# A hybrid attention layer on one core: VectorE scales a tile's attention output at the head of the next tile's queue

## The chip, the core and the metric

The kernel runs on one core of one Trainium2 chip. Five engines work side by side, each through its own queue in order: TensorE (PE, matrix products and transposes; its weight loads are shown as PEld), VectorE (DVE), ScalarE (ACT), GpSimd (POOL), and SyncE (SP), which issues nearly all DMAs. They meet only at semaphores. The metric is the device time of one execution in microseconds (us), lower is better.

## The reference, cut to what matters

The layer takes 2048 tokens of width 1024. A first projection gives queries, keys, values and an indexer; the indexer scores every earlier key, each query keeps its 256 best, and eight heads of width 64 attend over those alone. A pooling mixer, an output projection, a squared-ReLU MLP and a gated embedding follow. The part around the change is:

```python
score = jnp.einsum('bqh,bqhs->bqs', wb, jax.nn.relu(logits))
score = jnp.where(causal[None], score, -jnp.inf)
_, sel = lax.top_k(score, n_keep)                 # n_keep = 256
...
s = jnp.einsum('bqgrd,bqkgd->bqgrk', qg, kg) * ATTN_SCALE
pr = jax.nn.softmax(s, axis=-1)
o = jnp.einsum('bqgrk,bqkgd->bqgrd', pr, vg)      # attention output
mix = jnp.concatenate([attn_out, pool_out], axis=-1) @ w_o[i]
h = h + rmsnorm(mix, g_mix_post[i])
```

## The kernel before, in words

There are three stages, one after the other: the projection, the attention stage (about 427 to 1836 us of the trace) and the MLP with the rest. The change is in the attention stage.

The attention stage goes over 16 tiles of 128 queries, numbered i = 0 to 15. Tile i attends over its first 128(i+1) keys, cut into 1 block of keys for tiles 0 to 3, 2 for tiles 4 to 7, 3 for tiles 8 to 11 and 4 for tiles 12 to 15 (`blocks_of`). Each tile has eight heads; H = 8i + h counts them through. Every engine has its own loop over H, written out in full. There is no scheduler: the order of the code is the order of each queue.

For each head TensorE makes the scores of head H+2 or H+3 (lines 1455 and 1456, `exact_product`), turns the probabilities of head H block by block (line 1506, `turn_probs`), and multiplies them with the values (line 1520, `weigh`). All eight heads of a tile add their output into one bank of PSUM, bank 7. In head 0 of a tile it also turns the queries of the next tile (line 1468, `turn_queries`). Its product for block b stands one block behind the turn: turn 0, turn 1, weigh 0, turn 2, weigh 1 and so on; the last weigh of a head is behind the scores of head H+3.

Scores, turned queries and indexer products share a ring of three PSUM banks. An item can be written when the item three places before it was taken out (`wait_ring`). With three blocks or more per head, the scores of one head fill the ring, so the next item waits until VectorE has taken that head's first block out. The fourth block of head H+2 is the first ring item of head H; after it come, in head 0, the two halves of the turned queries.

VectorE takes the score blocks out with the mask added and their maximum (line 1112, `mask_head`), makes the negated maximum (line 1117), and splits the turned queries (line 1079, `split_queries`), before which TensorE can't make the scores that come next in the ring. In between VectorE and ScalarE search the threshold of the 256th best score for a pair of later tiles: 32 rounds of bisection per pair, three per head, from head 0 of an even tile to head 2 of the odd tile behind it (none in tiles 14 and 15). In a round VectorE counts for one tile (line 1131, `count_exact`) and ScalarE for the other (line 831, `count_below`), and then VectorE moves the threshold (lines 1139 to 1148, `move_threshold`; line 1129 prepares the next value). ScalarE does its first count behind its copy of the second turned block (line 880), or behind the first one where there is only one block.

`outputs(i)` is what the change moves. It waits for the last weigh of tile i (semaphore `pv_ps`), takes the reciprocal of the eight sums (line 1190), and scales bank 7 into `o_sb` (line 1192). Only then can TensorE write bank 7 for tile i+1: its first weigh of a tile waits for `o_rdy`. `o_sb` is turned in head 3. `scale_mix(i-2)`, in the same head 0, scales the output projection of the tile before last (line 1206); it waits for a root that GpSimd makes (line 680), and GpSimd's residual addition (line 689) waits for it.

Of the kernel before, what the change touches and what calls it, by code (L numbers as in the profile page):

```python
# [47 lines left out]
def hybrid_block(nc, x, p, positions, g_mix_pre, w_in, w_pool, pool_scale, w_o, g_mix_post,  # L48
# [29 lines left out]
    with ExitStack() as ctx:  # L78
# [276 lines left out]
        def turns_index(H):  # L355

            i, h = divmod(H, Q_HEADS)
            return (i + 3, i + 4) if i % 2 == 1 and h == 4 and i + 4 < T else ()
# [23 lines left out]
        for H in range(HEADS):  # L382
            i, h = divmod(H, Q_HEADS)
# [25 lines left out]
        def rounds_in(H):  # L409

            i, h = divmod(H, Q_HEADS)
            s = Q_HEADS * (i % 2) + h
            if i // 2 + 1 >= T // 2 or s > 10:
                return range(0)
            return range(min(3 * s, ROUNDS), min(3 * s + 3, ROUNDS))
# [24 lines left out]
        def over(cols, width):  # L440

            return cols.unsqueeze(2).to_broadcast([P, cols.shape[1], width])
# [537 lines left out]
        def _(dve):  # L980
# [93 lines left out]
            def split_queries(i):  # L1074
                low = slice(P // 2, P)
                for n in range(2):
                    dve.wait_ge(q_hi, 2 * i + n + 1)
                    part = q_parts[low, i % 2, 4 * n:4 * n + 4, :]
                    nc.vector.tensor_tensor(part, split4(bank[low, ring_bank("q", i, n), :]), part.bitcast(F32),  # L1079
                                            ALU.subtract).then_inc(ring_done, 1)  # L1080
# [22 lines left out]
            def mask_head(H):  # L1103

                i, h = divmod(H, Q_HEADS)
                if h == 0 and i >= FIRST_PICK:
                    dve.wait_ge(mask_rdy, i - FIRST_PICK + 1)
                if H >= 3:
                    dve.wait_ge(pT_ps, head_first[H - 2])
                for b, (o, w) in enumerate(blocks[i]):  # L1110
                    dve.wait_ge(ring_ps, ring[("s", H, b)] + 1)
                    nc.vector.tensor_tensor_reduce(out=probs[:, H % 3, o:o + w], in0=bank[:, ring_bank("s", H, b), 0:w],  # L1112
                                                   in1=mask[:, i % 2, o:o + w], scale=1.0, scalar=LEAST, op0=ALU.add,
                                                   op1=ALU.max, accum_out=block_max[:, H % 2, b:b + 1]).then_inc(ring_done, 1)
                nb = len(blocks[i])
                dve.wait_ge(ring_done, ring[("s", H, nb - 1)] + 1)
                nc.vector.tensor_reduce(neg_max[:, h:h + 1], block_max[:, H % 2, 0:nb], AX_X, ALU.max,
                                        negate=True).then_inc(negmax_rdy, 1)

            def start_search(t):  # L1120
                nc.vector.memset(threshold[:], 0).then_inc(thr_rdy, 1)
                dve.wait_ge(score_rdy, t - FIRST_PICK + 1)

            def count_exact(t, k):

                keys = P * (t + 1)
                dve.wait_ge(thr_rdy, tries(t) + k + 1)
                if k > 0:
                    nc.vector.tensor_scalar(next_tried[:], threshold[:], 2 ** (31 - k) // 2, None,
                                            ALU.bitwise_xor).then_inc(tried_rdy, 1)  # L1130
                nc.vector.tensor_scalar(kept[:, 0:keys], score[:, 0, 0:keys], threshold[:, 0:1].bitcast(F32), -float(P),  # L1131
                                        ALU.is_lt, ALU.add, accum_out=below[:, 0:1]).then_inc(exact_count, 1)

            def move_threshold(t, k):

                done = ROUNDS * (t // 2 - 1)
                dve.wait_ge(exact_count, done + k + 1)
                dve.wait_ge(act_count, done + k + 1)
                nc.vector.tensor_scalar(too_few[:], below[:], float(P * (t + 2) - 2 * KEEP), None,  # L1139
                                        ALU.is_gt).then_inc(few_rdy, 1)  # L1140
                dve.wait_ge(few_rdy, done + k + 1)
                if k == 0:
                    nc.vector.tensor_scalar(flip[:], too_few[:], -1.0, None, ALU.mult).then_inc(flip_rdy, 1)
                    dve.wait_ge(flip_rdy, t // 2)
                    nc.vector.tensor_scalar(threshold[:], flip[:], 1 << 30, None, ALU.bitwise_xor).then_inc(thr_rdy, 1)
                else:
                    dve.wait_ge(tried_rdy, (ROUNDS - 1) * (t // 2 - 1) + k)
                    nc.vector.scalar_tensor_tensor(out=threshold[:], in0=too_few[:], scalar=31 - k, in1=next_tried[:],  # L1148
                                                   op0=ALU.logical_shift_left, op1=ALU.bitwise_xor).then_inc(thr_rdy, 1)

            def settle(t):

                keys = P * (t + 1)
                dve.wait_ge(thr_rdy, tries(t) + ROUNDS + 1)
                nc.vector.tensor_scalar(kept[:, 0:keys], score[:, 1, 0:keys], threshold[:, 1:2].bitcast(F32), 0.0,
                                        ALU.is_gt, ALU.add, accum_out=above[:, 1:2]).then_inc(settle_step, 1)
                nc.vector.tensor_scalar(next_up[:], flip[:, 1:2], 2.0, 1.0, ALU.mult, ALU.add).then_inc(settle_step, 1)
                dve.wait_ge(settle_step, 2 * (t // 2))
                nc.vector.scalar_tensor_tensor(out=toggled[:], in0=above[:, 1:2], scalar=float(KEEP), in1=next_up[:],
                                               op0=ALU.is_ge, op1=ALU.mult).then_inc(settled, 1)  # L1160
# [26 lines left out]
            def outputs(i):  # L1187
                dve.wait_ge(pv_ps, head_first[Q_HEADS * (i + 1)])
                dve.wait_ge(oT_ps, i)
                nc.vector.reciprocal(inv_denom[:], denom[:, i % 2, :]).then_inc(invden_rdy, 1)  # L1190
                dve.wait_ge(invden_rdy, i + 1)
                nc.vector.tensor_tensor(o_sb[:], bank[:, 7, :].rearrange("p (h d) -> p h d", d=HEAD),
                                        over(inv_denom[:], HEAD), ALU.mult).then_inc(o_rdy, 1)
# [5 lines left out]
            def scale_mix(i):  # L1199
                dve.wait_ge(rstdB_rdy, 2 * i + 1)  # L1200
                dve.wait_ge(h2_st, 16 * i)
                if i == 0:
                    dve.wait_ge(wo_ld, 16 * (K + 1))
                for n in range(2):
                    cols = slice(n * 512, (n + 1) * 512)
                    nc.vector.scalar_tensor_tensor(out=h2_t[:, cols], in0=bank[:, n, :], scalar=rstdB[:, 0:1],
                                                   in1=g_post_row[:, cols], op0=ALU.mult, op1=ALU.mult).then_inc(h2_scaled, 1)
# [19 lines left out]
            for H in range(HEADS):  # L1227
                i, h = divmod(H, Q_HEADS)
                rounds = rounds_in(H)
                first = 2 * (i // 2) + 2  # L1230
                if len(rounds) and rounds[0] == 0:
                    start_search(first)
                if len(rounds):
                    count_exact(first, rounds[0])
                if H + 2 < HEADS:
                    mask_head(H + 2)
                if h == 0 and i >= 1:
                    outputs(i - 1)
                if h == 0 and i >= 2:
                    scale_mix(i - 2)  # L1240
                for k in rounds:
                    if k != rounds[0]:
                        count_exact(first, k)
                    move_threshold(first, k)
                if i % 2 == 1 and h == 3 and i + 2 < T:
                    settle(i + 2)
                    select(i + 1)
                if i % 2 == 1 and h == 4 and i + 2 < T:
                    select(i + 2)
                if h == 0 and i + 1 < T:  # L1250
                    split_queries(i + 1)
                for t in turns_index(H):
                    split_index_queries(t)
                weigh_heads(index_share(H))
                if h == 1 and i >= 2:
                    residual_mean(i - 2)
                if h == 7 and i >= 1:
                    mix_mean(i - 1)
# [424 lines left out]
```

## Time and profile before

| | |
|---|---|
| time, median of 3 runs | 3635.95 us (3632.55 to 3638.81) |
| profiled execution | 3635.46 us, its span 3633.7 us |
| PE busy | 3153.3 us, 87% |
| DVE busy | 1671.5 us, 46% |
| ACT busy | 1314.5 us, 36% |
| POOL busy | 351.8 us, 10% |
| attention stage, 427 to 1836 us | PE 1064.08, DVE 906.76, ACT 719.03 us of 1409 |
| mean granted TensorE clock | 0.79 of full speed in the attention stage, 0.98 behind it |

The shares are averages over the three stages. In the attention stage no engine is busy all the time; what is to be read there is who waits for whom around the start of each tile.

### The profile page before, as it was taken

How to read it: one execution, taken by the hardware profiler on the slowest of the kernel's cores; microseconds unless marked ns; L12 is line 12 of the kernel's file. 1: busy time of each engine (PE TensorE's matmuls, PEld its weight loads, DVE VectorE, ACT ScalarE, POOL GpSimd, SP SyncE). 2: the span in 40 equal slices, each digit the busy share in tenths (PEclk: the TensorE clock that was granted, in tenths of full speed). 3: DMA queues.
4: the chain of work that ended last, by engine and by line, in shares of the span. 5: the costliest groups of instructions: out<-in, count | busy, mean ns of one | idle time of the engine just before them, and what ended most of it. 6: DMA issues, size and time to landing. Idle time of an engine off the chain costs nothing.

```text
span 3633.7 us, 38370 instructions
## 1 busy us (share of the span) xinstructions
PE 3153.3 (87%) x13944; PEld 2422.5 (67%) x13944; DVE 1671.5 (46%) x3354; ACT 1314.5 (36%) x2130; POOL 351.8 (10%) x457
## 2 busy tenths in 40 slices
PE   5999667677777777788869999999999999999998
PEld 4888545455565666667658885688857888478873
DVE  3221277767677777752133334333343333433333
ACT  3222255637373746633332222222223222232221
POOL 1323311120303012000000000000000000000000
PEclk9999867777878878788889999999999999999999
DMA  3111211110101000000053332233313333032210
GB/s 111 52 52 52 93 41 38 43 36 27 33 27 32 12 27 27 21 21 21 27 191 116 94 103 72 75 121 100 122 35 105 99 98 122 29 121 94 93 58 23
DMA packets 211405, 241.93 MB, mean 67 GB/s; under 512 B 57504, under 2 KB 158368, under 8 KB 211232
## 3 DMA queue, kind: packets, MB, share of 16 engines
q1 hardware_dynamic: 208928, 231.27, 20.1%
q10 hardware_dynamic: 2304, 8.39, 0.6%
q8 instruction: 104, 1.70, 0.2%
q14 instruction: 69, 0.57, 0.1%
HBM read 203.98 MB, written 35.65 MB: 66 GB/s over the span
## 4 chain that ended last, share of the span: by engine, by line
issue 54%; PE 25%; DVE 10%; ACT 7%; POOL 2%; DMA 1%; SPq 0%; DVEq 0%; POOLq 0%; ACTq 0%
PE bank L1409 9%; PE bank L1538 6%; PE bank L1520 4%; DVE kept L1131 3%; ACT drop L831 2%; PE bank L1455 2%; ACT probs L865 2%; PE bank L1456 2%; PE bank L1506 1%; POOL score L700 1%; ACT probsT L880 1%; DVE kept L1178 1%; DVE too_few L1139 1%; DVE probs L1112 1%; DVE threshold L1148 1%
## 5 line engine op out<-in xcount | busy, mean ns | idle before, releaser
L1274 DVE TENSOR_TENSOR w_lo<-w_raw,w_hi 128x1024 fp32r<-128x1024 f32 x256 | 312.7, 1222 | 522.2 <-ACT w_hi L923 516.5
L1520 PE MATMUL bank<-values,probsT 128*128 128x64 f32 x2176 | 368.6, 322 | 130.4 <-ACT probsT L880 125.7
L1520 PEld LDWEIGHTS bank<-values,probsT 128*128 128x128 f32 x2176 | 354.1, 239 | 176.4 <-ACT probsT L880 163.6
L923 ACT CAST w_hi<-w_raw 128x1024 fp32r<-128x1024 f32 x256 | 267.3, 1044 | 563.1 <-PE bank L1409 535.0
L1409 PE MATMUL bank<-hn_hi,w_hi 128*128 128x512 f32 x1024 | 401.0, 392 | 16.1 <-DVE hn_lo L1291 10.9
L1409 PE MATMUL bank<-w_hi,hid_lo 128*128 128x512 f32 x1024 | 406.4, 397 | 0.0
L1409 PE MATMUL bank<-w_lo,hid_hi 128*128 128x512 f32 x1024 | 406.4, 397 | 0.0
L1409 PE MATMUL bank<-w_hi,hid_hi 128*128 128x512 f32 x1024 | 406.4, 397 | 0.0
L1409 PE MATMUL bank<-hn_lo,w_hi 128*128 128x512 f32 x1024 | 400.1, 391 | 0.0
L1409 PE MATMUL bank<-hn_hi,w_lo 128*128 128x512 f32 x1024 | 400.0, 391 | 0.0
L880 ACT COPY probsT<-bank 128x384 f32<-128x384 f32 (+3 forms) x320 | 163.6, 518 | 558.6 <-PE bank L1506 558.2
L831 ACT ACTIVATE drop<-score,threshold 128x512 bf16<-128x512 f32 (+6 forms) x224 | 305.5, 1364 | 89.7 <-DVE threshold L1148 66.0
L1131 DVE TENSOR_SCALAR_CACHE_REDUCE kept<-score,threshold 128x384 f32<-128x384 f32 (+6 forms) x224 | 315.1, 1407 | 1.0
L1455 PE MATMUL bank<-k_hi,q_parts 128*128 128x384 f32 (+3 forms) x320 | 170.0, 531 | 148.1 <-DVE q_parts L1079 87.5
L1112 DVE CUSTOM_DVE_ANT_0 probs<-bank,mask 128x384 f32<-128x384 f32 (+3 forms) x320 | 183.5, 607 | 149.2 <-PE bank L1456 148.4
L1538 PE MATMUL bank<-wo_sb,mixT_t 128*128 128x512 f32 x512 | 245.9, 632 | 0.7 <-ACT mixT_t L837 0.7
L1409 PEld LDWEIGHTS bank<-hn_hi,w_hi 128*128 128x128 f32 x1024 | 193.1, 189 | 58.0 <-issue 17.5
L1655 PE MATMUL bank<-w_gate_sb,h3T 128*128 128x512 f32 x512 | 226.8, 602 | 0.0
L1409 PEld LDWEIGHTS bank<-w_hi,hid_hi 128*128 128x128 f32 x1024 | 193.2, 189 | 46.6
L1409 PEld LDWEIGHTS bank<-w_lo,hid_hi 128*128 128x128 f32 x1024 | 193.2, 189 | 46.6
L1409 PEld LDWEIGHTS bank<-w_hi,hid_lo 128*128 128x128 f32 x1024 | 193.2, 189 | 46.6
L1309 DVE CAST hid_hi<-square 128x512 fp32r<-128x512 f32 x128 | 54.6, 427 | 365.3 <-ACT square L948 365.3
(173 smaller groups left out, 4610.5 us busy)
## 6 DMA issues: line engine op xcount, KB each, us to landing
w_raw<-in_w_up SPq DMA_DIRECT2D x64, 1024.0 KB, 5.5
w_raw<-in_w_down SPq DMA_DIRECT2D x64, 1024.0 KB, 5.0
x_in<-in_x SPq DMA_DIRECT2D x16, 512.0 KB, 4.6
q_t<-q_scratch SPq DMA_DIRECT2D x32, 256.0 KB, 3.7
x_t<-in_x SPq DMA_DIRECT2D x16, 512.0 KB, 4.3
h_scratch<-h_t SPq DMA_DIRECT2D x16, 512.0 KB, 3.1
hnT_scratch<-hn2T_t SPq DMA_DIRECT2D x16, 512.0 KB, 3.5
hn_lo<-hnT_scratch SPq DMA_DIRECT2D x4, 2048.0 KB, 11.8
```

The source lines that it names most:

```text
L831: nc.scalar.activation(drop[:, 0:keys], score[:, 1, 0:keys], ACT.Sign, scale=-1.0, bias=threshold[:, 1:2].bitcast(F32), accum_out=below[:, ...
L865: nc.scalar.activation(span, span, ACT.Exp, bias=neg_max[:, h:h + 1], accum_out=denom[:, i % 2, h:h + 1]).then_inc(exp_rdy, 1)
L880: nc.scalar.copy(probsT[:, m % 2, 0:w], bank[:, 5 + m % 2, 0:w]).then_inc(pT_ev, 1)
L923: nc.scalar.copy(w_hi[:, p % 4, :].rearrange("p (k f) -> p k f", f=piece_width(p)), raw_piece(p)).then_inc(w_hi_rdy, 1)
L1112: nc.vector.tensor_tensor_reduce(out=probs[:, H % 3, o:o + w], in0=bank[:, ring_bank("s", H, b), 0:w], in1=mask[:, i % 2, o:o + w], scale= ...
L1131: nc.vector.tensor_scalar(kept[:, 0:keys], score[:, 0, 0:keys], threshold[:, 0:1].bitcast(F32), -float(P), ALU.is_lt, ALU.add, accum_out=b ...
L1274: nc.vector.tensor_tensor(out_p, raw_piece(p), hi_p.bitcast(F32), ALU.subtract).then_inc(w_lo_rdy, 1)
L1409: ins = nc.tensor.matmul(dst, lhs[a], rhs[b], start=(first and n == 0), stop=(last and n == 2))
L1455: nc.tensor.matmul(dst, q, k_hi[:, key, o:o + w], start=True, stop=False)
L1520: last = nc.tensor.matmul(bank[:, 7, h * HEAD:(h + 1) * HEAD], probsT[:, m % 2, a * P:(a + 1) * P], values[:, kt, HEAD * kv:HEAD * (kv + 1 ...
L1538: last = nc.tensor.matmul(bank[:, n, :], mixT_t[:, k, :], wo_sb[:, k, n * 512:(n + 1) * 512], start=(k == 0), stop=(k == K - 1))
L1655: last = nc.tensor.matmul(bank[:, (2, 4)[n], :], h3T[:, a % 2, k, :], w_gate_sb[:, k, n * 512:(n + 1) * 512], start=(k == 0), stop=(k == K ...
```

## The change

In head 0 of each tile from tile 1 on, `outputs(i - 1)` is issued ahead of the first count and of the masked maxima of head H+2, where it was issued behind them. The final `outputs(15)` and every other engine's queue stay as they are.

```diff
                 if len(rounds) and rounds[0] == 0:
                     start_search(first)
+                if h == 0 and i >= 1:
+                    outputs(i - 1)
                 if len(rounds):
                     count_exact(first, rounds[0])
                 if H + 2 < HEADS:
                     mask_head(H + 2)
-                if h == 0 and i >= 1:
-                    outputs(i - 1)
                 if h == 0 and i >= 2:
                     scale_mix(i - 2)
                 for k in rounds:
```

This is VectorE's queue at the start of tile 10, an even tile with three blocks of 384, 512 and 512 keys. The rows with a minus and a plus are the same work, in its place before and now; h_t stands for the tile of the residual stream.

```order
 L1197 TENSOR_SCALAR msB<-ssB 128x1
 L1121 MEMSET threshold 128x2
-L1131 TENSOR_SCALAR kept,below<-score,threshold 128x1664
-L1112 ISA probs,block_max<-bank,mask 128x384
-L1112 ISA block_max 128x1
-L1117 TENSOR_REDUCE neg_max<-block_max 128x1
...
 L1190 RECIPROCAL inv_denom<-denom 128x8
 L1192 TENSOR_TENSOR o_sb<-bank,inv_denom 128x512
+L1131 TENSOR_SCALAR kept,below<-score,threshold 128x1664
+L1112 ISA probs,block_max<-bank,mask 128x384
```

The reciprocal and the scaling now stand ahead of the count of 1664 scores and of the three blocks of head 82.

In tile 14 there is no search. VectorE's queue at its start is now:

```order
1897 L1197 TENSOR_SCALAR msB<-ssB 128x1
1898 L1190 RECIPROCAL inv_denom<-denom 128x8
1899 L1192 TENSOR_TENSOR o_sb<-bank,inv_denom 128x512
1900 L1112 ISA probs,block_max<-bank,mask 128x384
1901 L1112 ISA block_max 128x1
1902 L1112 ISA probs,block_max<-bank,mask 128x512
1903 L1112 ISA block_max 128x1
```

Rows 1898 and 1899 stood behind the four blocks of head 114 and their negated maximum, and stand ahead of them now.

TensorE's queue at the same place, which the change leaves as it was. The first row is the last weigh of tile 13, the third the fourth score block of head 114, the fifth the queries of tile 15:

```order
1677 L1520 MATMUL bank<-values,probsT 128x64 x4
1678 L1506 MATMUL bank<-ident,probs 128x128 x3
1679 L1455 MATMUL bank<-k_hi,q_parts 128x512
1680 L1456 MATMUL bank<-k_lo,q_parts 128x512
1681 L1468 MATMUL bank<-ident,q_t 128x128 x8
1682 L1506 MATMUL bank<-ident,probs 128x128 x4
1683 L1520 MATMUL bank<-values,probsT 128x64 x3
```

Nothing moved here: rows 1679 and 1681 wait for ring banks that line 1112 empties, row 1683 for `o_sb`.

## Rows read from the trace of the kernel before

**Rows 1.** The page: the group of line 1112; busy us, mean ns, idle before.

```profile
L1112 DVE CUSTOM_DVE_ANT_0 probs<-bank,mask 128x384 f32<-128x384 f32 (+3 forms) x320 | 183.5, 607 | 149.2 <-PE bank L1456 148.4
```

**Rows 2.** The tile inv_denom: durations in ns (least, median, most), and who waited.

```profile
L1190 DVE RECIPROCAL inv_denom<-denom x16: 202/203/204, 481.2 to 1796.2; 128x8 f32<-128x8 f32 x16
L1192 DVE TENSOR_TENSOR o_sb<-bank,inv_denom x16: 691/692/692, 481.4 to 1796.4; 128x512 f32<-128x512 f32 x16
...
  PE bank L1520: 3.0, 4
```

**Rows 3.** Who waited for whom: us in total, times, longest.

```profile
PE bank L1455 <- DVE q_parts L1079: 87.5, 16, 7.9
```

**Rows 4.** Timeline, start of tile 10: start, us busy, engine, line; in brackets the idle time before.

```profile
1166.37 1.00 PE L1520 MATMUL bank<-values,probsT 128*128 128x64 f32 x8
1166.01 1.95 DVE L1131 TENSOR_SCALAR_CACHE_REDUCE kept<-score,threshold 128x1664 f32<-128x1664 f32 x1
1168.59 1.17 PE L1468 MATMUL bank<-ident,q_t 128*128 128x128 f32 x8 [0.89 <-DVE block_max L1112]
1170.02 0.69 DVE L1192 TENSOR_TENSOR o_sb<-bank,inv_denom 128x512 f32<-128x512 f32 x1
1170.62 1.40 DVE L1206 SCALAR_TENSOR_TENSOR h_t<-bank,rstdB,g_post_row 128x512 f32<-128x512 f32 x2
1172.10 2.35 POOL L689 TENSOR_TENSOR h_t<-h_t,x_t 128x1024 f32<-128x1024 f32 x1 [1.84 <-DVE h_t L1206]
1172.71 1.77 DVE L1139 TENSOR_SCALAR too_few<-below 128x2 int32<-128x2 f32 x1 [0.69 <-ACT drop L831]
```

**Rows 5.** Timeline, starts of tiles 8, 12 and 4.

```profile
972.54 1.00 PE L1520 MATMUL bank<-values,probsT 128*128 128x64 f32 x8
972.29 1.68 DVE L1131 TENSOR_SCALAR_CACHE_REDUCE kept<-score,threshold 128x1408 f32<-128x1408 f32 x1
975.76 0.69 DVE L1192 TENSOR_TENSOR o_sb<-bank,inv_denom 128x512 f32<-128x512 f32 x1
976.57 1.41 DVE L1206 SCALAR_TENSOR_TENSOR h_t<-bank,rstdB,g_post_row 128x512 f32<-128x512 f32 x2
...
1383.70 1.00 PE L1520 MATMUL bank<-values,probsT 128*128 128x64 f32 x8
1383.46 2.21 DVE L1131 TENSOR_SCALAR_CACHE_REDUCE kept<-score,threshold 128x1920 f32<-128x1920 f32 x1
1392.20 0.78 DVE L1139 TENSOR_SCALAR too_few<-below 128x2 int32<-128x2 f32 x1 [1.67 <-ACT drop L831]
...
645.86 1.00 PE L1520 MATMUL bank<-values,probsT 128*128 128x64 f32 x8
646.27 1.15 DVE L1131 TENSOR_SCALAR_CACHE_REDUCE kept<-score,threshold 128x896 f32<-128x896 f32 x1
649.95 1.41 DVE L1206 SCALAR_TENSOR_TENSOR h_t<-bank,rstdB,g_post_row 128x512 f32<-128x512 f32 x2 [0.66 <-POOL rstdB L680]
```

**Rows 6.** Timeline, start of tile 13.

```profile
1505.17 0.67 DVE L1139 TENSOR_SCALAR too_few<-below 128x2 int32<-128x2 f32 x1 [1.78 <-ACT drop L831]
```

**Rows 7.** Timeline, starts of tiles 14 (three rows) and 15.

```profile
1609.27 0.56 DVE L1112 CUSTOM_DVE_ANT_0 probs<-bank,mask 128x384 f32<-128x384 f32 x1 [3.60 <-PE bank L1456]
1610.63 1.25 PE L1520 MATMUL bank<-values,probsT 128*128 128x64 f32 x8
1614.60 0.85 PE L1520 MATMUL bank<-values,probsT 128*128 128x64 f32 x6 [0.62 <-DVE o_sb L1192]
...
1710.38 1.08 PE L1520 MATMUL bank<-values,probsT 128*128 128x64 f32 x8 [1.49 <-DVE o_sb L1192]
```

**Rows 8.** Stretches of tiles 12 and 15: engine times, granted clock (1.00, 0.50), DMA.

```profile
1385.00:1386.20 1.20, 0.03 (x1) 0.00 (x0) 1.20 (x5) 1.13 (x2) 1.06 (x2) 0.86 0.00 0
1386.20:1388.00 1.80, 1.79 (x6) 1.49 (x7) 1.45 (x5) 1.02 (x2) 1.43 (x3) 0.50 0.00 0
1710.40:1712.00 1.60, 1.60 (x15) 1.60 (x16) 1.15 (x2) 0.74 (x4) 0.38 (x1) 1.00 0.00 0
```

## The prediction

> **What bounds the kernel now.** I read the waits first, then the timeline around the start of every tile. All durations are from the profiled execution: span 3633.7 us, device time 3635.46 us, 0.5 below the median of 3635.95. The sum is a difference, so I add it to the median.
>
> The product that the change wants to release is the first weigh of a tile. TensorE waited for `o_sb` 4 times, 3.0 us in all [rows 2]; that is the whole prize. The large wait at the same place is another: for the split queries, 16 times, 87.5 us, the longest 7.9 [rows 3]. In head 0 VectorE splits them behind all three rounds of the search, so until then TensorE stands, whatever happened to bank 7. The start of a tile is therefore paced by VectorE's queue, with ScalarE's counts in it, and a delay of that queue shifts both engines alike. I find no idle time behind it that would take the delay up: an even tile is paced by the search up to the next start, and an odd tile begins with TensorE waiting for VectorE again. I count a delay of the threshold as a delay of the end.
>
> **What the change adds.** No instruction comes or goes. The reciprocal (203 ns) and the scaling (692 ns) [rows 2] take about 0.85 us of the queue: in tile 8 the scaling starts at 975.76, the next work 0.61 later if it didn't wait (tile 10: 1170.02 to 1170.62), and the reciprocal stands 0.24 ahead [rows 4, 5]. What changes is when they may start: VectorE must now wait for the last weigh of the previous tile before it counts or takes a score block out. Queued behind that wait are the first count, the masked blocks of head H+2 and, through them, TensorE's next ring items, its second turned block, ScalarE's copy of it and ScalarE's first count.
>
> *Even tiles 8, 10 and 12.* VectorE comes there just behind the indexer work, before TensorE has weighed. With W the end of the last weigh, the count starts at W + 0.85 instead of at its old time [rows 4, 5]:
> - tile 10: 1167.37 + 0.85 - 1166.01 = 2.21 late;
> - tile 8: 973.54 + 0.85 - 972.29 = 2.10;
> - tile 12: 1384.70 + 0.85 - 1383.46 = 2.09.
>
> 0.85 of that is given back where `outputs` stood before, so line 1206 is 1.36 late in tile 10 and 1.24 in tile 12; in tile 8 it is 1.25 less the 0.20 that it waited (975.76 + 0.61 against 976.57), 1.05. The residual addition follows it. In tile 10 the small operation of line 1139 took 1.77 us instead of its usual 0.17 and ended at 1174.48, with GpSimd's addition (1172.10 + 2.35) [rows 4]: it stood as long as the addition ran. So the threshold moves with the addition: +1.36 in tile 10, +1.05 in tile 8. In tile 12 ScalarE's count is later still: line 1139 began at 1392.20 behind it, now 1392.20 + 2.09 + 0.17 = 1394.46 against an end at 1392.98 [rows 5]: +1.48. Sum of the three: 3.9.
>
> *Even tiles 2, 4 and 6.* In tile 4 the shift is 646.86 + 0.85 - 646.27 = 1.44; less 0.85 and less the 0.66 us that line 1206 waited for the root [rows 5] nothing is left. Line 1139 slips from just ahead of the addition to behind its start, which costs one step of 0.2 us after it. The same in tile 6; in tile 2 there is one block and ScalarE's count doesn't hang on it. Together 0.4.
>
> *Odd tiles.* VectorE comes late, TensorE waits for it, and the last weigh is long done: nothing is waited for. But the blocks of head H+2 are taken out 0.85 us later, and with them ScalarE's first count. In tiles 1 to 9 GpSimd's addition, or the single block, covers it. In tile 13 it doesn't: 1505.17 + 0.85 + 0.17 = 1506.19 against 1505.84 [rows 6], +0.35. Tile 11 is alike, 0.4. Together 0.8.
>
> *Tiles 14 and 15* have no search, and TensorE is the bound. Before, VectorE began on head 114's blocks at 1609.27. Now it waits for the weigh that ends at 1611.88 and begins at 1612.73 [rows 7]. At 0.61 us a block [rows 1] the third is out at about 1614.6; only then can TensorE turn the second half of the queries (half of 1.17 us, [rows 4]), turn block 1 (some 0.45) and weigh, near 1615.7 against 1614.60: +1.1, though its wait of 0.62 for `o_sb` is gone. In tile 15 no queries are turned; TensorE loses about 1.4 us at the fourth score block and gets back the 1.49 that it waited for `o_sb` [rows 7]: 0.
>
> Sum: 3.9 + 0.4 + 0.8 + 1.1 = 6.2 us.
>
> *The clock.* TensorE's waits for a ring bank become longer in tiles 8, 10 and 14: 0.89 us in tile 10 [rows 4] becomes 3.1. In tile 12 the granted clock read 0.86 in 1.2 us without work and 0.50 (1.2 GHz) in the stretch behind; in tile 15, behind 1.49 us of waiting, it stayed at 1.00 (2.4 GHz) [rows 7, 8]. At the lower level the turns and products up to ScalarE's first count take twice as long. That costs at least nothing and at most about 0.4 in tile 8, 0.75 in tile 10 (there 0.5 is hidden behind the addition) and 1.5 in tile 14, estimates by doubling what took 1.17 in tile 10 and its neighbours: 0 to 2.65, and I take 1.2, between two rows that fell either way.
>
> The Trainium skill ("TensorE: Matmul & The Clock Gate", Part 1: The HAM clock gate) says that the hardware's sampling runs free of the kernel, so that where the clock changes varies from run to run. The two unlike rows agree with it. By that page this term would differ between runs, within the same 0 to 2.65.
>
> The Trainium skill ("SBUF — State Buffer", SBUF: two separate sides) says that VectorE and GpSimd take a shared port pair in turn, the loser being blocked for the whole instruction, if VectorE's instruction runs in a 2-port mode or has two SBUF inputs. In tiles 4 to 12 the moved pair now falls beside GpSimd's additions of indexer heads. The scaling has one input in PSUM. If the reciprocal were blocked by that rule, each such start would lose up to one more addition. The sixteen reciprocals took 202 to 204 ns without exception, tile 4's among them, and it ran beside such an addition: I price it at nothing.
>
> Forecast: 6.2 + 1.2 = 7.4 us, 3635.95 + 7.4 = **3643.3 us**, slower by 0.20%.
>
> **The rivals.**
>
> *Not slower: the early release pays, the wait doesn't.* The mechanism is the residual addition. If in tiles 8 to 12 it were held by something other than line 1206, as in tile 4 by GpSimd's root, the threshold would come at its old time and the 3.0 us of waits for `o_sb` would be gained: 3635.95 - 3.0 = 3633. It decides at a slack of 1.25 us ahead of line 1206 in those tiles; the rows show 0.20 in tile 8 and none in tiles 10 and 12. The waits of 87.5 us speak against it also: they stand behind the gain. Ten in a hundred, and it is hardly a measurable gain even then.
>
> *Absorbed in part.* The delays are real, but the search or TensorE recovers within the tile, for instance through the copies of ScalarE; then tile 14 and half of the rest stay, about 1.1 + 2.5 = 3.6: 3639.5. For it: in tiles 12 and 13 ScalarE copies between counts, so the search there isn't a pure chain. Against: the query split stands behind it all. Thirteen in a hundred.
>
> *The clock falls more widely.* Longer waits leave TensorE at 1.2 GHz in tiles 14 and 15, where it is the bound, and the full 2.65 comes: with two more such stretches of about 1.5, 6.2 + 2.65 + 3 = 12: 3648. Seven in a hundred.
>
> That the change doesn't do what it says: `o_sb` is ready early, but in a tile of several blocks TensorE can't weigh earlier, since the ring holds it ahead of its second turn. That is part of my forecast.
>
> **How the numbers follow.** The forecast has 70 in a hundred, with 3641 to 3646 as its own range. A measurement of this kernel can tell about 0.2%, 7.3 us, from no change, and my forecast lies on that line. Of its 70, 43 lie beyond the line, since the clock term and unlisted delays only add. With the wide clock case that makes 0.51 slower. The rest of the forecast (27), the absorbed case (13) and most of the not slower case make 0.46 the same; 0.03 is left for faster. The range runs from 3638 to 3649: it leaves out the not slower case and the far end of the last.
>
> **What would show it.** In the new profile the reciprocal waits for line 1520 at the start of the even tiles, about 1.4 us in tiles 8, 10 and 12, and in tile 14. TensorE's 3.0 us for `o_sb` are gone, and its waits for `block_max` at lines 1455 and 1468 are up by several us. The wait for the split queries keeps its 16 times. Line 1206 is 1.0 to 1.4 us later against the count's old start in tiles 8 to 12. The attention stage is 6 to 9 us longer and the MLP as long as before. I am wrong if those starts shift by less than half of what I list, or if the stage ends no later.

## The result, and the profile after

The change makes the kernel slower by 0.24%: 3641.26 us (median of 20 runs) against 3632.5 us of the kernel before, measured beside it (20 runs). The ratio is 1.0024, 95% interval 1.0017 to 1.0031, that is 6.2 to 11.3 us. The prediction was 7.4 us more, a ratio of 1.0020. Its 3643.3 us started from a median of three runs that lay 3.5 us higher than the one of twenty.

The page of the changed kernel, from its profiled execution (3640.07 us): the span and the engines' busy time.

```profile
span 3638.2 us, 38364 instructions
## 1 busy us (share of the span) xinstructions
PE 3162.6 (87%) x13944; PEld 2432.0 (67%) x13944; DVE 1662.0 (46%) x3354; ACT 1314.5 (36%) x2130; POOL 351.8 (10%) x457
```

The span is up by 4.5 us, and every engine runs as many instructions as before. What moved are waits. DVE is busy 9.5 us less, about half of it at line 1139 (see turn_first). That PE is busy 9.3 us longer says nothing of the change: it was 3161.0 in a repeat of the kernel before. The tile `inv_denom` in the changed kernel, the counterpart of [rows 2], now with the lines that say what VectorE waited for ahead of the tile's instructions:

```profile
its engine sat idle before it (us, times) until:
  PE bank L1520: 18.3, 3
  issue: 6.1, 5
who waited for it (us, times):
```

TensorE waits for `o_sb` nowhere any more. In its place VectorE waits for line 1520 ahead of the reciprocal, 18.3 us in 3 places: tiles 14 and 15, where it used to wait for TensorE a little later anyway, and the last `outputs`, which the change leaves alone. The five waits put down to "issue" are those of the even tiles 4 to 12 (0.81, 0.71, 1.48, 1.59 and 1.47 us); the timeline below shows for tile 10 that such a wait too ends with the last weigh. Two of TensorE's waits in the changed kernel:

```profile
PE bank L1455 <- DVE q_parts L1079: 79.9, 16, 7.5
PE bank L1468 <- DVE block_max L1112: 35.0, 8, 7.0
```

The wait for the split queries still comes at every tile [rows 3]; it is 7.6 us smaller, while the wait one step earlier, at the ring, is 10.9 us larger: 35.0 us for `block_max` at line 1468, which was 24.1 before. I read this as the same time spent one step earlier.

Tile 10 in the timeline of the changed kernel, the counterpart of [rows 4]:

```profile
1168.99 0.20 DVE L1197 TENSOR_SCALAR msB<-ssB 128x1 f32<-128x1 f32 x1
1169.70 1.00 PE L1520 MATMUL bank<-values,probsT 128*128 128x64 f32 x8
1170.79 0.20 DVE L1190 RECIPROCAL inv_denom<-denom 128x8 f32<-128x8 f32 x1 [1.59 <-issue]
1171.63 1.94 DVE L1131 TENSOR_SCALAR_CACHE_REDUCE kept<-score,threshold 128x1664 f32<-128x1664 f32 x1
1174.20 1.94 PE L1468 MATMUL bank<-ident,q_t 128*128 128x128 f32 x8 [3.17 <-DVE block_max L1112]
1175.40 1.41 DVE L1206 SCALAR_TENSOR_TENSOR h_t<-bank,rstdB,g_post_row 128x512 f32<-128x512 f32 x2
1176.89 2.36 POOL L689 TENSOR_TENSOR h_t<-h_t,x_t 128x1024 f32<-128x1024 f32 x1 [3.32 <-DVE h_t L1206]
1177.51 1.79 ACT L831 ACTIVATE drop<-score,threshold 128x1792 bf16<-128x1792 f32 x1
1179.50 0.17 DVE L1139 TENSOR_SCALAR too_few<-below 128x2 int32<-128x2 f32 x1 [2.69 <-ACT drop L831]
1185.03 1.30 DVE L1079 TENSOR_TENSOR q_parts<-bank,q_parts 64x512 fp32r<-64x512 f32 x2
```

VectorE is free at about 1169.2, the last weigh ends at 1170.70, and the reciprocal starts at 1170.79. The count, the ring (TensorE waits 3.17 us where it waited 0.89), line 1206 and ScalarE's count all follow later. To compare it with before, two more rows of the kernel before are needed, its arrival at tile 10 (line 1197) and its split of the queries:

```profile
1165.66 0.20 DVE L1197 TENSOR_SCALAR msB<-ssB 128x1 f32<-128x1 f32 x1
...
1179.84 0.69 DVE L1079 TENSOR_TENSOR q_parts<-bank,q_parts 64x512 fp32r<-64x512 f32 x1
```

From arrival to split the start of the tile took 1179.84 - 1165.66 = 14.18 us, and takes 1185.03 - 1168.99 = 16.04: **1.86 us more**. I measured every start in this way. What lies between one split and the next arrival I call the stretch between. In the first pair of profiles the starts sum to +7.4 us and the rest, up to the arrival at tile 15, to some -4.3. The result therefore hangs on what the stretches are.

Tile 14 in the changed kernel, the counterpart of [rows 7]:

```profile
1611.55 1.00 PE L1520 MATMUL bank<-values,probsT 128*128 128x64 f32 x8
1612.59 0.20 DVE L1190 RECIPROCAL inv_denom<-denom 128x8 f32<-128x8 f32 x1 [6.26 <-PE bank L1520]
1614.05 0.50 PE L1455 MATMUL bank<-k_hi,q_parts 128*128 128x512 f32 x1 [1.16 <-DVE block_max L1112]
1616.20 0.78 PE L1520 MATMUL bank<-values,probsT 128*128 128x64 f32 x6
```

TensorE now stands 1.16 us for the ring ahead of the fourth score block. From the last weigh of tile 13 to the first of tile 14 it took 3.97 us (1610.63 to 1614.60) and takes 4.65; in the repeats of both kernels it is 3.72 and 4.65.

Tile 15 in the changed kernel:

```profile
1709.29 1.37 PE L1520 MATMUL bank<-values,probsT 128*128 128x64 f32 x8
1712.28 0.50 PE L1455 MATMUL bank<-k_hi,q_parts 128*128 128x512 f32 x1 [1.18 <-DVE block_max L1112]
1713.28 1.00 PE L1520 MATMUL bank<-values,probsT 128*128 128x64 f32 x8
```

From the last weigh of tile 14 to the first of tile 15 it is 3.99 us; before, it was 4.00 (1706.38 to 1710.38). The wait of 1.49 us for `o_sb` is gone and one of 1.18 for the ring stands in its place.

### The profile page after: what moved, and what is told of

Its sections match the earlier page's. It is cut to its first block, busy times and chain, and to the rows that moved or that the text cites. A ratio compares the mean times of both kernels' runs of the same rounds, so it can differ in the third digit from the quotient of the medians.

```text
span 3638.2 us, 38364 instructions
## 1 busy us (share of the span) xinstructions
PE 3162.6 (87%) x13944; PEld 2432.0 (67%) x13944; DVE 1662.0 (46%) x3354; ACT 1314.5 (36%) x2130; POOL 351.8 (10%) x457
## 4 chain that ended last, share of the span: by engine, by line
issue 54%; PE 25%; DVE 10%; ACT 7%; POOL 2%; DMA 1%; SPq 0%; DVEq 0%; POOLq 0%; ACTq 0%
PE bank L1409 9%; PE bank L1538 6%; PE bank L1520 4%; DVE kept L1131 3%; ACT drop L831 3%; PE bank L1455 2%; ACT probs L865 2%; PE bank L1506 2%; PE bank L1456 2%; ACT probsT L880 1%; POOL score L700 1%; DVE kept L1178 1%; DVE too_few L1139 1%; DVE probs L1112 1%; DVE threshold L1148 1%
## 5 line engine op out<-in xcount | busy, mean ns | idle before, releaser
L946 ACT ACTIVATE square<-bank 128x512 f32<-128x512 f32 x128 | 76.5, 598 | 403.8 <-PE bank L1409 403.8
```

The costliest lines, as they stand in the source:

```text
L946: nc.scalar.activation(square[:, f % 2, :], bank[:, UP[q % 2][f % 2], :], ACT.Relu).then_inc(relu2_step, 1)
```

## The experiments

The table gives, for each run with a profile, how much longer each start took than in the first profile of before, in us. It is worked out as above, from lines 1197 and 1079 of each trace; starts 2, 3, 7 and 9 are at 0.0 in every run, but for turn_first with -0.2 in 7 and 9.

| start of tile | forecast | after | after_again | before_again | count_first | even_only | weigh_first | weigh_first_before | turn_first |
|---|---|---|---|---|---|---|---|---|---|
| 4 | 0.2 | 0.19 | 0.19 | 0.02 | 0.01 | 0.20 | -0.01 | 0.00 | 0.01 |
| 5 | 0 | 0.21 | 0.19 | -0.01 | 0.01 | 0.14 | 0.20 | 0.00 | 0.00 |
| 6 | 0.2 | 0.23 | 0.20 | 0.04 | 0.23 | 0.20 | 0.23 | 0.04 | 0.03 |
| 8 | 1.05 + clock | 1.29 | 1.28 | 0.01 | 0.02 | 1.27 | 0.00 | 0.01 | 0.96 |
| 10 | 1.36 + clock | 1.86 | 1.86 | -0.01 | 0.00 | 1.84 | 0.18 | 0.00 | 1.25 |
| 11 | 0.4 | 0.39 | 0.40 | -0.01 | 0.40 | -0.02 | 0.39 | 0.00 | -0.22 |
| 12 | 1.48 | 1.57 | 1.75 | -0.45 | 0.19 | 1.64 | 0.06 | -0.44 | 1.15 |
| 13 | 0.35 | 0.74 | 0.73 | 0.01 | 0.74 | 0.01 | -0.30 | -0.29 | -0.20 |
| 14 | 1.1 + clock | 0.88 | 0.88 | 0.01 | 0.87 | 0.84 | 1.19 | 1.43 | 0.44 |
| all starts | 6.2 + 1.2 | 7.4 | 7.5 | -0.4 | 2.5 | 6.1 | 1.9 | 0.8 | 3.0 |
| the rest, up to tile 15 | 0 | -4.3 | -3.8 | -4.6 | -5.2 | -2.6 | -5.4 | -0.2 | -1.4 |
| of it, ahead of the arrival at tile 2 | 0 | 0.0 | -1.4 | -3.4 | -1.0 | -0.9 | -0.6 | -1.0 | -3.6 |

The rest is the shift of the arrival at tile 15 less the sum of the starts: the stretches between, and all that lies ahead of tile 2.

### before_again and after_again: do the parts repeat?

Both kernels once more, unchanged, each with one time and one profile.

> The kernel before once more, for a second profile. In the two profiles so far each tile can be cut in two: the start, from VectorE's arrival (line 1197 of the tile before) to its split of the queries, and the stretch from there to the next arrival. The starts account for +7.4 us of the change, the stretches between for -4.2 us. Theory (drift is the clock's chance): this run differs from the first by less than 0.3 us in the sum over the starts, but by 2 to 5 us in single sums over the stretches, up or down. Rival (the stretches really gain from the change): stretches repeat within 1 us too.

> The changed kernel once more, for a second profile. Theory: the starts repeat, +7.4 us within 1 against the first profile of before (the clock may change tiles 8, 10 and 14 by some tenths), and the stretches between them come out at another value than -4.2. Rival (a real gain in the stretches behind the starts, that takes more than half of the loss back): the stretches come out near -4.2 again.

Measured: 3632.33 us and 3640.53 us. The starts repeat to 0.1 us except at tile 12. The rest doesn't repeat: the kernel before gave -4.6 us against its own first profile, as much as the changed kernel gave against it. So a figure of -4.3 from one pair shows no gain from the change. The profiles alone don't exclude one either. The changed kernel's -3.8 is near the first -4.2, as the rival said, and behind the arrival at tile 2 the two profiles of the changed kernel read -4.2 and -2.4, those of the kernel before 0 and -1.2. What decides is the timing: 6.2 to 11.3 us of loss against 7.4 in the starts leaves at most about 1.3 us to be given back. The rival, that more than half comes back, falls by that. The attention stage of the changed kernel ends 3.1 us later (3.6 for its repeat) against the first profile of before and 6.7 us (7.2) against the second.

What varies is TensorE's clock, at least where I could see it: in the start of tile 12 the same eight turns of queries took 1.91 us in the first profile of before and 1.06 in the second.

```profile
1387.23 1.91 PE L1468 MATMUL bank<-ident,q_t 128*128 128x128 f32 x8
```

```profile
1380.84 1.06 PE L1468 MATMUL bank<-ident,q_t 128*128 128x128 f32 x8
```

The first row is of the first profile, the second of its repeat; the granted clock over these turns was 0.50 in the first and 1.00 in the second. At the higher level that start was 0.45 us shorter, though nothing was edited. This weighs on every figure for tile 12 in the table: both profiles of the changed kernel ran these turns in 1.91 us. Against the repeat of before, that start lost 2.0 and 2.2 us and not 1.57 and 1.75.

### count_first: the wait covered by the count

```diff
                 if len(rounds):
                     count_exact(first, rounds[0])
+                if h == 0 and i >= 1:
+                    outputs(i - 1)
                 if H + 2 < HEADS:
                     mask_head(H + 2)
-                if h == 0 and i >= 1:
-                    outputs(i - 1)
```

> The output is taken out behind the first count, but still ahead of the masked blocks. The count of 0.9 to 2.2 us covers the wait for the last weigh in the even tiles. Theory (the loss is VectorE's wait for the last weigh with all that is queued behind it): starts of tiles 4 to 12 even lose nothing or up to 0.3 us each, tiles 11 and 13 lose 0.4 as in the change, tile 14 (no count to cover the wait) 0.9; in sum about 2 us, ratio 1.0005. Rival (the loss is the order itself, the score blocks taken out behind 0.85 us more of work): the even starts lose about 0.9 us each, in sum 5 us or more, ratio 1.0015 or more.

Measured: 3635.44 us, ratio 1.0003 (0.9994 to 1.0012). The starts of tiles 8 and 10 lose 0.02 and 0.00 us, tile 12 loses 0.19; tiles 11, 13 and 14 keep what they lost in the change. The sum is 2.5 us. In tile 10 no wait stands ahead of the scaling. The last weigh ended at 1164.89, while the count was still running:

```profile
1163.54 1.95 DVE L1131 TENSOR_SCALAR_CACHE_REDUCE kept<-score,threshold 128x1664 f32<-128x1664 f32 x1
1165.64 0.69 DVE L1192 TENSOR_TENSOR o_sb<-bank,inv_denom 128x512 f32<-128x512 f32 x1
```

The order, blocks taken out 0.85 us later, is in this run as in the change; the wait is not. In tiles 8 and 10 the loss is the wait, and for them the rival (0.9 us each from the order) falls. In tile 12 the turns took 1.91 us, so against the repeat of before 0.6 us of about 2.0 remains. Where nothing was waited for, in tiles 11 and 13, and in tile 6, the loss is still there: that part is the order, as forecast. Tile 8 also shows that a lower clock by itself can be free: its turns took 1.94 us here against 1.06 before, and its start lost 0.02.

### even_only: the change in tiles 2, 4 to 14 alone

```diff
+                early_out = i % 2 == 0
+                if h == 0 and i >= 1 and early_out:
+                    outputs(i - 1)
                 ...
-                if h == 0 and i >= 1:
+                if h == 0 and i >= 1 and not early_out:
                     outputs(i - 1)
```

> The output is taken out early in tiles 2, 4 to 14 only; the odd tiles are as before. Theory: the even starts lose what they lost in the change (0.2, 0.2, 1.3, 1.9, 1.6, 0.9 for tiles 4 to 14), the odd ones nothing, 6 us in sum, ratio 1.0016. Rival (an early release helps wherever the wait is short, so the odd half hides a gain): odd starts come out faster in the change than here, and this one is slower than the change, ratio above 1.0024.

Measured: 3640.29 us, ratio 1.0018 (1.0009 to 1.0027). The even starts 8 to 14 lose what they lost in the change, tiles 11 and 13 nothing: 6.1 us. Tile 5 still lost 0.14, though its order is as before. By the starts the odd half costs about 1.2 us and hides no gain; the times, with 1.0018 here and 1.0024 in the change, can't tell the two kernels apart.

### weigh_first, and its control weigh_first_before

```diff
+                if h == Q_HEADS - 1:
+                    weigh(H, nb - 1)
                 scores(H + 3, early(H + 3))
-                weigh(H, nb - 1)
+                if h < Q_HEADS - 1:
+                    weigh(H, nb - 1)
```

> The changed kernel, and in addition TensorE weighs the last block of a tile's last head ahead of the scores of head H+3, not behind them (head 7 of each tile only; the other heads as before). Theory (the even starts lose because the last weigh ends after VectorE's arrival): the reciprocal no longer waits for line 1520 or nearly so in tiles 8, 10 and 12, and the starts' loss there falls from 1.3, 1.9 and 1.6 us to under 0.5 each; tile 14's 0.9 falls too. What TensorE itself loses by waiting for ScalarE's copy ahead of that weigh comes in the stretches. Rival (the loss is the order on VectorE): the starts keep their loss.

> The same edit of TensorE's order on the kernel before: the control for the run above. Both theories: starts as in the kernel before within 0.3 us each; its stretches show what the earlier weigh costs TensorE by itself.

Measured: 3637.87 us, ratio 1.0012 (1.0003 to 1.0021), for the first; 3637.26 us, a single time, for the control, 3.0 above the median of before. With TensorE's last weigh ahead of the scores of head H+3 (three blocks in these tiles), the starts of tiles 8, 10 and 12 fall to 0.00, 0.18 and 0.06 us (against the control to -0.01, 0.18 and 0.50, its turns in tile 12 having run in 1.06 us and not in 1.91). VectorE's queue is that of the changed kernel:

```profile
1165.65 0.20 DVE L1197 TENSOR_SCALAR msB<-ssB 128x1 f32<-128x1 f32 x1
1165.78 0.20 DVE L1190 RECIPROCAL inv_denom<-denom 128x8 f32<-128x8 f32 x1
1166.01 0.69 DVE L1192 TENSOR_TENSOR o_sb<-bank,inv_denom 128x512 f32<-128x512 f32 x1
```

The reciprocal follows the arrival by 0.13 us, where it was 1.80 in the change. That takes the cause away from the other side: the same order of VectorE, no wait, and little or no loss. Two things came out against what I expected. Tile 14 didn't fall: it is 1.19, and 1.43 in the control, so it is the edit of TensorE's order that costs there. And the control was to keep its starts within 0.3 us, where tile 12 took 0.44 less and tile 14 1.43 more.

### turn_first: ScalarE's count freed of the ring

```diff
                 for b in range(nb):
-                    turn_probs(H, b)
+                    if not (h == 0 and b == 1):
+                        turn_probs(H, b)
                     if b == 0:
+                        if h == 0 and nb > 1:
+                            turn_probs(H, 1)
                         scores(H + 2, late(H + 2))
```

> The changed kernel, and in addition in head 0 TensorE turns block 1 of the probabilities ahead of the fourth score block and of the queries, which wait for a ring bank. ScalarE's first count then hangs neither on the masked blocks nor on TensorE's clock. Theory (two parts: VectorE late with line 1206 and so the residual addition, and ScalarE late through the ring and the clock): the first part stays, 1.05, 1.4 and 1.25 us in tiles 8, 10 and 12 and 0.2 in tiles 4 and 6; the second goes, so tiles 11 and 13 lose nothing. Sum of the starts about 4 us instead of 7.4. Rival (all of it comes through ScalarE's late count): the starts lose less than 1 us in all; other rival (the addition holds everything): tiles 8, 10 and 12 keep 1.3, 1.9 and 1.6.

Measured: 3637.42 us, ratio 1.0009 (1.0000 to 1.0018). The starts of tiles 8, 10 and 12 keep 0.96, 1.25 and 1.15 us of 1.29, 1.86 and 1.57; tiles 5, 11 and 13 lose nothing or gain 0.2. The sum is 3.0, where I expected 4; the 0.2 that tiles 4 and 6 were to keep went too. What tiles 8, 10 and 12 keep is the forecast's first part: line 1206 late and with it the residual addition (forecast 1.05, 1.36, 1.24). Both rivals fall.

The edit also gains something by itself: tiles 7 and 9, which lost nothing in the change, gain 0.2. It was not run alone on the kernel before, but the trace shows the step. ScalarE's count is out so early that line 1139 runs ahead of the residual addition, and the operation behind it stands beside the addition in its place (line 1143, 2.35 us in tile 8). So the difference to the change, 0.3, 0.6 and 0.4 us, is about 0.2 too large for what came through the ring, the clock and ScalarE's copy. The ends of the residual addition say the same. Counted from the arrival it is 1.15, 1.48 and 1.36 us later in the change than before in tiles 8, 10 and 12, which leaves 0.1, 0.4 and 0.2 of the losses.

Why a count that is over 3 us late costs so little shows in tile 8, first in the kernel before, then in the changed one:

```profile
978.06 2.35 POOL L689 TENSOR_TENSOR h_t<-h_t,x_t 128x1024 f32<-128x1024 f32 x1 [1.52 <-DVE h_t L1206]
978.18 2.25 DVE L1139 TENSOR_SCALAR too_few<-below 128x2 int32<-128x2 f32 x1 [0.20 <-ACT drop L831]
```

```profile
982.31 2.36 POOL L689 TENSOR_TENSOR h_t<-h_t,x_t 128x1024 f32<-128x1024 f32 x1 [2.67 <-DVE h_t L1206]
984.65 0.17 DVE L1139 TENSOR_SCALAR too_few<-below 128x2 int32<-128x2 f32 x1 [2.42 <-ACT drop L831]
```

Before, line 1139 came early and stood until the addition was over. In the change it came as the addition ended and took 0.17 us. The count ends 3.4 us later, counted from the arrival, but 2.1 us of that had been spent standing beside the addition before; 1.3 is left, which is what the start lost.

### queries_early: the large wait of the same place

```diff
 # VectorE, head 0
                 if h == 0 and i >= 1:
                     outputs(i - 1)
+                if h == 0 and i + 1 < T:
+                    split_queries(i + 1)
                 if h == 0 and i >= 2:
                     scale_mix(i - 2)
                 ...
-                if h == 0 and i + 1 < T:
-                    split_queries(i + 1)
 # ScalarE, head 0, behind the first copy and exponentials
+                        if h == 0 and i + 1 < T:
+                            split_queries(i + 1)
```

ScalarE's own `split_queries` at the end of its head 0 goes too.

> The kernel before, but in head 0 ScalarE copies the turned queries right behind its first exponentials and VectorE splits them behind the masked blocks and the output, ahead of the three rounds of the search. Theory (the wait of 87.5 us for the split is the real loss of the tile's start): TensorE's wait for q_parts falls under 35 us and the time falls by 10 to 40 us. Rival (even tiles are paced by the search on VectorE and ScalarE, so the wait only moves to block_max at a later head): the wait falls, the waits for block_max rise by as much, and the time stays within 5 us.

Measured: 3592.36 us, ratio 0.9882 (0.9867 to 0.9897), 42 us faster and a little more than the range I gave. TensorE's 87.5 us for the split queries [rows 3] are 1.4 us in one place, and its waits for `block_max` at line 1455 rose only from 35.5 to 44.5 us. About half of the 86 us came back as time. A large part of the other half stands at line 1520, where TensorE's waits for ScalarE's copy of the probabilities (line 880) rose from 125.7 to 172.4 us. In tile 10 the split stands at 1147.14, 5.1 us behind the arrival, where it was 14.2:

```profile
1142.06 0.20 DVE L1197 TENSOR_SCALAR msB<-ssB 128x1 f32<-128x1 f32 x1
1147.14 1.30 DVE L1079 TENSOR_TENSOR q_parts<-bank,q_parts 64x512 fp32r<-64x512 f32 x2
```

The rival, that the search paces the tiles and the wait only moves, falls.

### qe_output_first, qe_count_first and qe_turn_first: the same questions on the faster kernel

Each is queries_early with the order of the change, of count_first or of turn_first.

> The run before (queries split early) with the output taken out first, as in the change. Theory: the wait for the last weigh delays VectorE in tiles 8, 10, 12 and 14 as it did in the change, so it is slower than the queries split early alone (3592.4 us), by 3 to 9 us: 3596 to 3601. Rival: with the large wait gone TensorE profits from an early release of bank 7 (it waits 5.5 us in 8 places for it there), and the time is 3587 to 3592.

> Queries split early, and the output taken out behind the first count and ahead of the masked blocks. Theory: no wait in tiles 2 to 12, so it costs nothing there, and it can give back some of the 5.5 us that TensorE waits for the output; tile 14 loses about 1: 3588 to 3594. Rival (the score blocks taken out 0.85 us later hold TensorE at the ring in each tile): 3595 to 3600.

> Queries split early, and in head 0 TensorE turns block 1 of the probabilities ahead of the fourth score block and of the queries. ScalarE's first count comes earlier, but the queries are turned 0.5 to 1 us later. Theory (the search paces the even and the first heads of the odd tiles): where VectorE waited for ScalarE's count this gains some tenths a tile, 3588 to 3592. Rival (the split of the queries, now later, is still what TensorE waits for): 3592 to 3598.

Measured: 3608.65 us (ratio to before 0.9935, 0.9915 to 0.9955), 3601.28 us (0.9917, 0.9900 to 0.9933) and 3595.62 us (0.9898, 0.9881 to 0.9914). Against queries_early they lose 16, 9 and 3 us by the medians. The kernel before, timed beside them, was 1.6 us faster than beside queries_early; by the ratios they lose about 19, 13 and 6. I expected 3 to 9 us for the first. There TensorE waits for `o_sb` nowhere, yet it waits longer at the ring than in queries_early: 35.0 us against 25.7 at line 1468. For qe_count_first and qe_turn_first the rival was nearer: the first came out a little beyond the rival's range and the second inside it, where the theory had expected about the time of queries_early. My explanation, argued and not shown, is that the query split is now near the head of VectorE's queue and TensorE goes on as soon as it comes, so 0.85 us ahead of it is no longer covered by ScalarE's counts. It can be only a part: against queries_early, the starts together take 9.2 us more in qe_output_first and 2.4 in qe_count_first, and what lies behind them I have not taken apart. None of the three beats queries_early, which has the lowest median of all the kernels here; from qe_turn_first the intervals don't separate it (0.9867 to 0.9897 against 0.9881 to 0.9914).

## Why the prediction was right

- **The prize was 3.0 us and none of it counted.** TensorE's waits for `o_sb` went to nothing, as said, and no start of a tile became shorter.
- **The added wait in tiles 8, 10 and 12.** Forecast 1.05, 1.36 and 1.48 us; measured 1.29, 1.86 and 1.57. count_first and weigh_first remove the wait in two different ways, and both bring the starts of tiles 8 and 10 to 0.2 or less. This is shown. Tile 12 goes the same way, but how far depends on the clock in the profile that one compares with: 0.2 and 0.1 remain against the first profile of before, 0.6 and 0.5 against its repeat. The forecast of 1.48 was built on the profile with the lower clock, and that 1.57 lies so close to it is in part luck.
- **The path of that loss.** Line 1206 and the residual addition are enough for most of it: with ScalarE's count freed of the ring, 0.96, 1.25 and 1.15 us stay (turn_first), and the addition ends 1.15, 1.48 and 1.36 us later. In one point the path was not the one of the forecast. It had the threshold of tiles 8 and 10 move with the addition alone. In the changed kernel line 1139 takes 0.17 us in all three tiles, behind ScalarE's count, and ends 0.15, 0.41 and 0.23 us later than the addition. Two paths are late there by nearly the same time; the one through ScalarE ends last, and freeing it alone wins back only the small difference.
- **Tiles 2, 4 and 6:** 0.4 forecast, 0.4 measured.
- **Odd tiles:** 0.8 forecast, 1.3 measured. Tile 11 came out at 0.39 as forecast. Tile 5 lost 0.2 where I had forecast nothing, and tile 13 0.74 instead of 0.35. The losses of tiles 11 and 13 go when ScalarE's count is freed of the ring, so their path is the one I named. The second 0.4 us of tile 13 lie in the row that the forecast started from. In the first profile of before ScalarE's count began 6.84 us behind the arrival, the clock having risen to 1.00 just before it; in the repeat it was still 0.50 and the count began at 7.24, hidden behind the addition in both. In the changed kernel it began at 8.08, which is 0.84 later than the repeat. In tile 5 it is the addition itself that is 0.2 late, and turn_first leaves it so; there only the 0.2 that its edit gains hides it.
- **Tiles 14 and 15:** 1.1 forecast for tile 14, 0.88 measured. For tile 15 I forecast no loss, 1.4 us at the fourth score block against 1.49 for `o_sb`. Measured between the weighs it is none: 3.99 us against 4.00, with 1.18 us of waiting in place of 1.49. The repeat of before took 3.84 there.
- **The clock term.** 1.2 us taken. In tiles 8 and 10 the clock fell as the forecast allowed. In tile 10 the stretch behind the long wait was granted near the lower level, 1.2 GHz, where the kernel before had 2.4 (1.00). Two rows of the changed kernel, the wait and what followed:

```profile
1170.50:1174.00 3.50, 0.53 (x5) 0.29 (x4) 3.18 (x7) 1.94 (x3) 2.85 (x4) 1.00 0.00 0
1174.00:1177.00 3.00, 2.80 (x14) 2.83 (x14) 2.78 (x9) 0.00 (x0) 0.11 (x1) 0.53 0.00 0
```

  The turns took 1.94 us there against 1.17 [rows 4], 1.7 times as long and not twice. In tile 14 the clock did not fall to the lower level (the turns took 1.18 us), so its 1.5 us did not come. Over tiles 8 and 10 the excess over turn_first is 0.33 + 0.61 = 0.9 us, and over the lateness of the addition about 0.5. Either is an upper bound for the clock, since ScalarE's copy and the ring are in it too. So this was the term of the sum that was mis-sized: 1.2 taken, 0.5 to 0.9 at most seen.
- **That the sum of the starts is 7.4, as forecast, is luck.** The clock came out some 0.7 us under its term and tile 14 0.2 under; the three even tiles came out some 0.3 over it and the odd tiles 0.5.
- **Rigid passing-on.** I counted each delay of a start as a delay of the end. The timing bears it out within its interval: 6.2 to 11.3 us for starts of 7.4. The rivals lie outside it: not slower, 3.6 us (absorbed in part) and 12 (the clock that falls more widely). A single pair of profiles would not have shown it. The attention stage was to be 6 to 9 us longer; in the first pair it ends 3.1 us later, against the repeat of before 6.7. Where the 1.4 us between 7.4 and the measured 8.8 stand, or whether they are noise, is open.

The Trainium skill ("TensorE: Matmul & The Clock Gate", Part 1: The HAM clock gate) says that the place where the clock changes varies from run to run. The two profiles of the kernel before agree: 1.91 and 1.06 us for the same turns of tile 12. Whether the clock is also what moves the stretches between was not measured.

## What to carry to other kernels

An engine's queue pays for the wait of its first instruction with everything behind it, so ask when the data is ready before asking who wants it: here the consumer's prize was 3 us, and moving the instruction ahead of work that used to cover the producer's last 1.5 us cost 7.4 us over the starts, 8.8 in time. One instruction further back, behind a count of 0.9 to 2.2 us, the same move cost a third of that over the starts, and nothing clear of noise in time. And at a busy place look at the largest wait first: the query split, a few lines away in the same queues, was worth 42 us.

## What the runs showed of the hardware that was not expected

- Cut at fixed instructions, parts of a program repeat very differently between executions. The starts of tiles repeated within 0.1 us in all but tile 12. All that lies outside them, up to tile 15, summed to 4.6 us of difference between two profiles of one kernel, 3.4 of it ahead of tile 2. A difference of 0.2% is then read from the parts that repeat, and from many timed runs, not from two spans.
- A VectorE operation on 128x2 values that takes 0.17 us stood for up to 2.25 us beside a GpSimd addition of 2.35 us, and ended within 0.05 us of it (tile 8, line 1139). When ScalarE's count came later, in the change, the same operation took 0.17 us again. So it is not only at semaphores that VectorE and GpSimd meet.
- Behind pauses of TensorE of no more than 0.68 and 1.18 us the granted clock read 0.50 in tile 12 of one profile of the kernel before, and 1.00 in its repeat, with pauses of 0.69 and 1.18 us.
- VectorE's waits for the last weigh in the even tiles 4 to 12 are listed under "issue" in the profile, and only the long ones, of tiles 14 and 15 and of the last `outputs`, under line 1520. The total of a named wait can leave out the very waits in question: 6.1 us in 5 places here.
